# ScalarE applies the norm's weights while it rounds, and VectorE makes the low half in one pass

## What is computed

```python
def rmsnorm(x, w):
    xf = x.astype(jnp.float32)
    y = xf * lax.rsqrt(jnp.mean(xf * xf, axis=-1, keepdims=True) + EPS)
    return (y * w.astype(jnp.float32)).astype(x.dtype)

# layer 0:  rmsnorm(x, e_norm)  @ e_w_in
# layer 1:  rmsnorm(x, o_norm)  @ o_w_in
# layer 2:  rmsnorm(rmsnorm(x, final_norm), norm_mix_w) @ w_in
# layer 3:  rmsnorm(h, norm_ffn_w) @ ffn_w_up
```

## Time and profile before

| | us |
|---|---|
| median of 3 runs | 3475.65 (3473.97 to 3477.48) |
| the profiled execution | 3474.76, its span 3472.6 |
| PE busy | 3231.7 (93%) |
| VectorE busy | 2320.0 (67%) |
| ScalarE busy | 1833.2 (53%) |
| POOL busy | 687.3 (20%) |
| first norm with its blocks | from 13 to 48 us |
| norms of layers 1, 2 and 3 | 669 to 807, 1454 to 1597, 2669 to 2740 us |

### The profile page before, as it was taken

The page is one execution under the profiler, slowest core; times in us unless marked ns, Lnnn a source line. Parts: engine busy times, 40 slices in busy tenths (PEclk is TensorE's granted clock), DMA queues, the critical chain, the costliest instruction groups (busy, mean ns, idle before and its releaser), DMA issues.

```text
span 3472.6 us, 54222 instructions
## 1 busy us (share of the span) xinstructions
PE 3231.7 (93%) x21710; PEld 2944.0 (85%) x21710; DVE 2320.0 (67%) x3235; ACT 1833.2 (53%) x2370; POOL 687.3 (20%) x1118
## 2 busy tenths in 40 slices
PE   6999878999999899998998988998999999999998
PEld 6889878888888888887877877888999888888887
DVE  7655767656666776667666766666656788888544
ACT  5544667544665555654555444333444566666443
POOL 2000000010000000012676775776000100000000
PEclk9999988999999999999999999988999999999999
DMA  5435333555444445555433333333555555555554
GB/s 189 141 134 180 126 109 132 191 188 195 163 156 156 151 152 174 173 188 199 158 105 115 129 121 121 132 131 128 199 184 183 188 192 189 189 191 191 188 188 140
DMA packets 158046, 560.54 MB, mean 161 GB/s; under 512 B 17552, under 2 KB 25808, under 8 KB 157152
## 3 DMA queue, kind: packets, MB, share of 16 engines
q1 hardware_dynamic: 157792, 557.06, 47.6%
HBM read 550.64 MB, written 6.36 MB: 160 GB/s over the span
## 4 chain that ended last, share of the span: by engine, by line
PE 68%; DVE 12%; POOL 10%; ACT 6%; issue 3%; DMA 1%; DVEq 0%; ACTq 0%; POOLq 0%; SPq 0%
PE ps L555 68%; POOL TB L1906 5%; DVE WL L1309 3%; POOL PT L1906 2%; ACT WH L890 2%; POOL BX L1906 2%; ACT L880 1%; POOL BS L1906 1%; POOL SQ L1906 1%; DVE XV L1283 1%; DVE XC L1283 1%; DVE BS L1299 0%; DVE X L1283 0%; DMA RAW<-in_w 0%; ACT SQ L880 0%
## 5 line engine op out<-in xcount | busy, mean ns | idle before, releaser
L555 PE MATMUL ps<-XN,WH 128*128 128x256 f32 (+1 forms) x8864 | 1901.3, 308 | 54.2 <-DVE XN L1272 20.0
L890 ACT ACTIVATE WH<-RAW 128x1024 fp32r<-128x1024 f32 x1010 | 1065.1, 1058 | 1309.2 <-PE ps L555 1276.8
L1309 DVE TENSOR_TENSOR WL<-RAW,WH 128x1024 fp32r<-128x1024 f32 x1010 | 1260.9, 1253 | 518.7 <-ACT WH L890 512.4
L555 PEld LDWEIGHTS ps<-XN,WH 128*128 128x128 f32 x8864 | 1468.2, 197 | 144.8 <-issue 22.2
L555 PE MATMUL ps<-XN,WL 128*128 128x256 f32 x5120 | 1461.8, 285 | 0.0
L555 PEld LDWEIGHTS ps<-XN,WL 128*128 128x128 f32 x5120 | 999.8, 195 | 0.0
L555 PE MATMUL ps<-YS,WH 128*128 128x512 f32 (+1 forms) x1088 | 377.7, 392 | 31.6 <-DVE ZB L1272 29.4
L1906 POOL TENSOR_TENSOR RSB<-RSB,SQ 128x256 f32<-128x256 f32 x75 | 87.5, 1166 | 1244.1 <-ACT SQ L880 1243.1
L555 PE MATMUL ps<-YS,WL 128*128 128x256 f32 x1056 | 296.5, 281 | 0.0
L555 PEld LDWEIGHTS ps<-YS,WH 128*128 128x128 f32 x1088 | 203.9, 190 | 81.9 <-DVE ZB L1272 32.3
L1906 POOL TENSOR_TENSOR SQ<-SQ 128x256 f32<-128x256 f32 (+1 forms) x32 | 37.8, 1182 | 1129.5 <-ACT SQ L880 1127.5
(11 more groups left out here) (327 smaller groups left out, 3423.3 us busy)
## 6 DMA issues: line engine op xcount, KB each, us to landing
RAW<-in_w SPq DMA_DIRECT2D x1010, 512.0 KB, 3.3
CSB<-sums SPq DMA_DIRECT2D x64, 128.0 KB, 3.7
scratch<-X SPq DMA_DIRECT2D x2, 2048.0 KB, 7.8
X<-scratch SPq DMA_DIRECT2D x2, 2048.0 KB, 7.7
X<-in_x SPq DMA_DIRECT2D x4, 512.0 KB, 7.9
X<-in_x SPq DMA_DIRECT2D x1, 2048.0 KB, 7.9
out<-X SPq DMA_DIRECT2D x4, 512.0 KB, 2.6
WIF<-in_w_if SPq DMA_DIRECT2D x1, 576.0 KB, 14.3
```

The source lines that it names most:

```text
L555: return pe.e.matmul(dst, l, r, start=start, stop=stop, skip_group_check=True)
L890: act.e.activation(WH[:, w % NH, :], RAW[:, w % NB, :], ACT.Copy).then_inc(*act.one(("wh", w)))
L1309: dve.e.tensor_tensor(WL[:, w % NB, :], RAW[:, w % NB, :], WH[:, w % NH, :].bitcast(F32), SUB).then_inc(*dve.one(("wl", w)))
```

## The change

ScalarE reads x itself and multiplies by the norm's weights, a column of 128, as it rounds. VectorE then computes x times weight minus the high half in a single scalar_tensor_tensor. TMP and TMP0 are gone (X keeps its place), and so are the marks `xw` and `xf`; the new mark `xa` says that X has its sum. For layer 2 the product of final_norm and norm_mix is made once (FW), and the square of x times final_norm takes the weight as the square's scale. ScalarE waits for the vectors (CV) ahead of its first instruction, and in `norm0` for the tiles of x. `st1` waits for `xa` in place of `xw`. In `norm0`, VectorE's low half now stands at the step of its own tile; in `project` it stands one tile later, as before.

```diff
--- before.py
+++ after.py
@@ -361,6 +361,7 @@
         RST = fx("RST", 2)
         TRI = fx("TRI", 384)
         EPSC = fx("epsc", 1)
+        FW = fx("FW", 16)
         R0 = fx.at

 
@@ -370,7 +371,6 @@
         w1 = m.at
         m = Map(nc, w1 + 5120, end)
         X0 = v3(m("X0", 16 * 256), 16)
-        TMP0 = v3(m("TMP0", 512), 2)
         m = Map(nc, R0, end)
         XMS = [v3(m(f"XMS{i}", 4 * 512, F32R), 4) for i in range(2)]
         XCS = [v3(m(f"XCS{i}", 4 * 512, F32R), 4) for i in range(2)]
@@ -407,7 +407,7 @@
         RS2 = m("RS2", 256)
         SPT = [m(f"SPt{i}", 16) for i in range(3)]
         m = Map(nc, XT, end)
-        TMP = v3(m("TMP", 512), 2)
+        m.at += 2048
         X = v3(m("X", 16 * 256), 16)

 
@@ -526,6 +526,10 @@
             w = dict(SHP)[name]
             return CS[rows, SOFF[name] + c:SOFF[name] + c + (n or w)]

+        def norm_w(L, k):
+
+            return FW[:, k:k + 1] if L == 2 else cv(["e_norm", "o_norm", "", "norm_ffn"][L], k)
+
         ident, ones = cs("ident"), cs("ones")
         LAYER = {"e_w_in": 0, "o_w_in": 1, "w_in_2": 2, "ffn_w_up_2": 3}

@@ -889,24 +893,27 @@
                         act.wait_ge(*at("used", w - NH))
                     act.e.activation(WH[:, w % NH, :], RAW[:, w % NB, :], ACT.Copy).then_inc(*act.one(("wh", w)))

-            def square(key, n, acc, slot, x):
+            def square(key, n, acc, slot, x, scale=1.0):
                 if n == 0:
-                    fn(acc, x, ACT.Square, (*key, 0))
+                    fn(acc, x, ACT.Square, (*key, 0), scale=scale)
                 else:
                     if n > 2:
                         act.wait_ge(*at(key[0][:-1], key[1], n - 2))
-                    fn(SQ4[:, slot + n % 2, :], x, ACT.Square, (*key, n))
-
-            def norm_tile(L, k, x, tmp):
+                    fn(SQ4[:, slot + n % 2, :], x, ACT.Square, (*key, n), scale=scale)
+
+            def norm_tile(L, k, x):
+                fn(XN[:, k, 0:256], x[:, k, :], ACT.Copy, ("xh", L, k), scale=norm_w(L, k))
+                square(("sqr", L), k, RSB, 0, x[:, k, :])
                 if L == 2:
-                    act.wait_ge(*at("xf", L, k))
-                    square(("sq1r", L), k, RS1, 2, tmp[:, k % 2, :])
-                act.wait_ge(*at("xw", L, k))
-                fn(XN[:, k, 0:256], tmp[:, k % 2, :], ACT.Copy, ("xh", L, k))
-                square(("sqr", L), k, RSB, 0, x[:, k, :])
+                    square(("sq1r", L), k, RS1, 2, x[:, k, :], cv("final_norm", k))

             def norm0(k):
-                norm_tile(0, k, X0, TMP0)
+                act.wait_ge(*at(f"x0{k // 4}"))
+                norm_tile(0, k, X0)
+
+            def project(L, kind, n):
+                act.wait_ge(*at("xa", L, n))
+                norm_tile(L, n, X)

             def rsqrt(dst, src, n, *names):
                 fn(dst, src, ACT.Ln, bias=EPSC, scale=1.0 / n)
@@ -1045,7 +1052,7 @@
                     fn(YS1[:, 16 + 4 * h:20 + 4 * h, 0:256], HB, ACT.Copy, ("yhh", h))

             def eo(n, s):
-                norm_tile(1, n, X, TMP)
+                project(1, "eo", n)

             def dts(s):
                 if s == 0:
@@ -1092,7 +1099,7 @@
                     fn(YS2[:, 4 * g:4 * g + 4, 0:256], YB, ACT.Copy, ("y2h", g))

             def oo(n, s):
-                norm_tile(2, n, X, TMP)
+                project(2, "oo", n)

             def s5c(s):
                 lr, dt, mag, th, r, s1, c1, den, fr_, fi_ = P1
@@ -1225,7 +1232,7 @@
                     fn(MS[:, n, 0:256], VB[:, n % 2, :], ACT.Copy, ("msh", n))

             def wo(n, s):
-                norm_tile(3, n, X, TMP)
+                project(3, "wo", n)

             def up(i, s_, s):
                 vg, k = VG[i % 2], 43 * s_ + i
@@ -1256,6 +1263,7 @@
                 rsqrt(RSB, bank("nsum", 4)[:, 0:256], 2048, ("rs", 4))

             act.wait_ge(*at("eps"))
+            act.wait_ge(*at("cv"))
             walk(lambda t, k, a, b: None, unit, {
                 "norm0": norm0, "nend": nend, "nend2": nend2, "xm": xm, "k": k_, "v": v, "o": o, "gates": gates, "z": z,
                 "lruc": lruc, "xl": xl, "zl": zl, "ra": ra, "ix": ix, "tail": tail, "heads": heads, "eo": eo, "dts": dts,
@@ -1327,26 +1335,13 @@
                 for t in range(taps - 2, -1, -1):
                     stt(dst, src[:, t:t + 256], w(t), dst, MUL, ADD, *(names if t == 0 else ()))

-            def norm_rest(L, k, tmp):
+            def norm_rest(L, k, x):
                 dve.wait_ge(*at("xh", L, k))
-                rest(XN[:, k, :], tmp[:, k % 2, :], ("xn", L, k))
-
-            def norm_tile(L, k, x, tmp, w):
-                t = tmp[:, k % 2, :]
-                if L == 2:
-                    ts(t, x[:, k, :], cv("final_norm", k), None, MUL, None, ("xf", L, k))
-                    dve.wait_ge(*at("sq1r", L, k))
-                    ts(t, t, cv(w, k), None, MUL, None, ("xw", L, k))
-                else:
-                    ts(t, x[:, k, :], cv(w, k), None, MUL, None, ("xw", L, k))
-                if k:
-                    norm_rest(L, k - 1, tmp)
-                if k == 15:
-                    norm_rest(L, k, tmp)
+                stt(XN[:, k, 256:512], x[:, k, :], norm_w(L, k), XN[:, k, 0:256].bitcast(F32), MUL, SUB, ("xn", L, k))

             def norm0(k):
                 dve.wait_ge(*at(f"x0{k // 4}"))
-                norm_tile(0, k, X0, TMP0, "e_norm")
+                norm_rest(0, k, X0)

             def softplus_mid(t1, t2):
                 ts(t2, t1, 1.0, None, ADD, None)
@@ -1360,6 +1355,7 @@

             def consts():
                 dve.wait_ge(*at("cs"))
+                tt(FW, cv("final_norm", 0, 16), cv("norm_mix", 0, 16), MUL)
                 ts(TRI, cs("mask"), 0.0, None, ALU.is_ge, None)

             def xm(h, j, s):
@@ -1510,15 +1506,18 @@
                     dve.wait_ge(*at("yhh", h))
                     rest(YS1[:, 16 + 4 * h:20 + 4 * h, :], HB, ("ysh", h))

-            def project(L, kind, n, load, w):
+            def project(L, kind, n, load):
                 dve.wait_ge(*at("tile", kind, n))
                 dve.wait_ge(*at(load))
                 tt(X[:, n, :], X[:, n, :], bank(kind, n)[:, 0:256], ADD)
-                tt(X[:, n, :], X[:, n, :], bank(kind, n)[:, 256:512], ADD, ("free", kind, n))
-                norm_tile(L, n, X, TMP, w)
+                tt(X[:, n, :], X[:, n, :], bank(kind, n)[:, 256:512], ADD, ("free", kind, n), ("xa", L, n))
+                if n:
+                    norm_rest(L, n - 1, X)
+                if n == 15:
+                    norm_rest(L, n, X)

             def eo(n, s):
-                project(1, "eo", n, "x1", "o_norm")
+                project(1, "eo", n, "x1")

             def dt(s):
                 dve.wait_ge(*at("st1"))
@@ -1594,7 +1593,7 @@
                     rest(YS2[:, 4 * g:4 * g + 4, :], YB, ("y2", g))

             def oo(n, s):
-                project(2, "oo", n, "x2", "norm_mix")
+                project(2, "oo", n, "x2")

             def nend2():
                 dve.wait_ge(*at("rsa", 2))
@@ -1849,7 +1848,7 @@
                     rest(MS[:, n, :], VB[:, n % 2, :], ("ms", n))

             def wo(n, s):
-                project(3, "wo", n, "x3", "norm_ffn")
+                project(3, "wo", n, "x3")

             def ffn0():
                 dve.wait_ge(*at("rs", 3))
@@ -2017,7 +2016,7 @@
                 load(X, args["x"], "x1")

             def st1():
-                sp.wait_ge(*at("xw", 1, 15))
+                sp.wait_ge(*at("xa", 1, 15))
                 load(scratch, X, "st1")

             def csb(h):
```

## The result

The changed kernel takes 3466.27 us in the median of 8 runs (3464.04 to 3468.58); the kernel before, in 8 runs beside it, 3476.58 (3473.97 to 3477.48). The profiled execution of the changed kernel took 3468.58, the slowest of its eight; its span of 3466.8 is 5.8 us under that of before (3472.6). So this trace shows only a part of what the medians show.

The account below looks back on a forecast made before the run. PE was taken as the bound, full in three of four normalizations, leaving the start and two seams: 1.5 + 0.4 + 0.3 = 2.2 us, so 3472.6 for the profiled execution, median 3473.4, range 3469.5 to 3477.2.

Parts of the forecast that it names:

- what FW costs: One added product of 16 columns for normalization 2, some 0.2 us, at a point where VectorE waits anyway.
- (d): Rival: PE's half-clock stretches elsewhere shift with the start, either way, several us, 3467 to 3484; chance 0.08.
- The start: First normalization: earlier first matmul, new VectorE order and shorter units together bring 1.5 us, ends at 0.35 and 2.8.
- this first start: PE's first matmul comes at 12.6 instead of 13.00, some 0.35 to 0.4 us sooner.
- let the clock fall: First normalization: row 5 taken at half clock, unit 2 ending at 27.1; had the clock held, 26.1.
- block row 5: First normalization: it waits for XN 5 behind two WL (3.45 us together) and begins near 24.5.
- The steady loop: Units 3 to 6 of the first normalization: about 4.0 us each instead of 4.1, some 0.5 over four.
- The rule of the Trainium skill: VectorE's new instruction on even tiles waits out POOL's addition: a unit takes 4.07 us, the start sum is 1.2.
- The seam behind normalization 1: X's scratch store goes out 0.4 us earlier and PE's later idle shrinks by 0.4; bounds 0 and 0.4.
- The seam behind normalization 2: The chain shortens by near one microsecond, of which 0.3 us counts; bounds 0 and 0.3.
- Normalizations 1 to 3 stay full of matmuls: PE has no idle in these three stages, so VectorE's or ScalarE's savings there are off the path.
- VectorE's 36 us: Work VectorE loses over the kernel, 36 us less; off the path in the three full stages.

Follow-up runs that it names:

- e1: The kernel before with 16 unused columns (64 bytes) ahead of R0, no instruction changed: 3466.03 us, ratio 0.9971 to the kernel before.
- e2: The changed kernel with FW written over norm_mix in CV, so that R0 and all addresses stay as before: 3472.36 us.
- e9: The changed kernel with XN moved up 32 bytes and R0 192 in all: 3447.77 us, ratio 0.9921 to the kernel before.
- e4: The kernel before with 8 idle columns (32 bytes) ahead of R0: 3478.17 us, ratio 1.0008 to the kernel before.
- e5: The kernel before with 32 idle columns (128 bytes) ahead of R0: 3482.90 us, ratio 1.0018 to the kernel before.
- e10: The kernel before with WH, XN and everything from R0 on moved up 64 bytes, RAW and WL staying: 3475.16 us, ratio 1.0000.

## Why the prediction was wrong

**Failed: what FW costs.** The prediction said of the sixteen columns "One tiny product (16 columns) is added once, some 0.2 us", and the text ahead of it says that X keeps its place. It priced the instruction and not the bytes: it set the effect of the 64 bytes on PE's full stages at nothing, without a reason, and e1 measured them at 9.5 us of the 10.3. Each of its terms rests on PE's full stages keeping their length, "Whatever VectorE or ScalarE save or lose there is off the path". That is right of the engines beside PE, but the stages got shorter by PE itself. No rival holds this; (d), the half-clock stretches, was given 3467 to 3484 and not for this reason. The measured time lies under its low end too.

**The start: right in kind, too small, and partly luck.** PE's timeline of the changed kernel, its waits in the first norm and the first sum of squares:

```profile
23.96 0.51 PE L559 MATMUL ps<-XN,WH 128*128 128x256 f32 x2 [1.69 <-DVE XN L1291]
27.94 0.51 PE L559 MATMUL ps<-XN,WH 128*128 128x256 f32 x2 [0.84 <-DVE XN L1291]
...
44.69 0.67 PE L559 MATMUL ps<-RSB,CS 128*128 128x256 f32 x2 [1.72 <-POOL RSB L1905]
...
24.00:28.00 4.00, 3.16 (x25) 2.96 (x25) 3.72 (x4) 2.85 (x5) 0.74 (x2) 1.00 0.29 97
```

PE's first matmul is at 12.61 (12.6 forecast), but that is luck: it lies between 12.48 and 13.15 in the kernels with the change and between 12.73 and 13.12 in those without (13.00 in the trace of before), so the traces don't show the 0.35 to 0.4 us forecast. The sum of squares is 3.2 us earlier, where 1.5 were forecast; 0.4 of it is this first start, the rest two things. The clock is one: behind the idle 1.69 us it stays at 1.00, where it was 0.55 behind 2.02 us before; by the table above that is worth 1.0 us in the new order, as the prediction had priced it before it let the clock fall. It is no property of the change, since in e1, which has before's instructions, the clock also read 1.00 behind 2.01 us of idle. The other is block row 5, at 23.96 here and 23.80 in e2 where my walk had 24.5, and so 0.5 to 0.7 us sooner: the two WL ahead of it took 2.90 us and not 3.45, a stretched duration that I had carried over from the earlier trace rows. A unit takes 3.97 us ((39.85 - 23.96)/4) where I had said 4.0.

The steady loop, in the changed kernel's chain that ended last (start, us, what):

```profile
23.96 1.72 PE ps L559 x12
...
25.76 1.07 ACT WH L894
...
26.86 0.52 ACT XN L884
...
27.40 0.50 DVE XN L1291
...
27.94 1.71 PE ps L559 x12
```

It is the odd tile that closes it, 1.72 + 1.07 + 0.52 + 0.50 and the small gaps between, and not the even one beside POOL's addition. My walk had the two within 0.1 us of each other and picked the other. The rule of the Trainium skill on a port held for the whole length (page "SBUF — State Buffer", section "Who interferes with whom") would have made it 4.07 a unit; the instruction that it delays isn't on the path here, so 3.97 says nothing on it. What does agree with it is the product FW, with two inputs in SBUF: it lasts 717 ns for 16 columns and ends with POOL's addition beside it (44.58 and 44.56 us).

**The seam behind normalization 1: too large.** PE's timeline of the changed kernel, answering to the earlier trace rows:

```profile
825.97 0.36 PE L717 MATMUL ps<-CS,ZB 64*128 64x64 f32 x1 [5.22 <-DVE ZB L1307]
```

PE idles 5.22 us for 5.38, so 0.16 came back of 0.4. The store is issued earlier, but PE reaches this place earlier as well. The wait is 5.73 in e2 and 6.39 in e9, which have the change, and 5.15 in e1, which has not: the term is no larger than its scatter.

**The seam behind normalization 2: right.** POOL's last addition takes 0.74 us at 1589.26, against 1.69, and PE works on until the sum stands next, with no wait for POOL on its weight load, where it had waited 0.32 us. How much of that reached the end of the kernel no run shows by itself.

**Normalizations 1 to 3 stay full of matmuls:** right, as the stretches above show. VectorE's 36 us, 33.7 in fact, were worth nothing there: in e2, where the data stay, the three output projections differ from before by 0.1 us or less.

**Rival (d) is at work, beside the cause.** Between the sum of squares behind norm 2 and the stage of the gated products stand 5650 matmuls. They took 920 us before and in e1, 926 in the changed kernel's profiled execution, 923.5 in e2's. The rows, before and changed:

```profile
1596.00:2516.00 920.00, 823.72 (x5651) 749.55 (x5650) 594.81 (x835) 414.10 (x545) 558.92 (x1001) 0.93 0.41 138
```

```profile
1589.00:2515.00 926.00, 831.06 (x5652) 756.12 (x5651) 593.29 (x834) 413.80 (x545) 558.78 (x1002) 0.92 0.41 137
```

The granted clock is 0.92 for 0.93, PE busy 7.3 us longer over the same matmuls. One place shows it plainly: behind a wait of 3.00 us for ZS in both kernels, the same blocks run at the full clock before and at 0.70 in the changed kernel, which costs 2.1 us.

```profile
2469.50:2475.50 6.00, 6.00 (x53) 6.00 (x52) 2.17 (x4) 1.82 (x3) 0.00 (x0) 1.00 0.94 350
```

```profile
2467.00:2475.10 8.10, 8.10 (x51) 8.10 (x51) 1.92 (x4) 1.78 (x3) 0.00 (x0) 0.70 0.89 322
```

So this trace shows 5.8 us of gain and not 10; its execution also lies 2.3 us over the median. From the sum of squares behind norm 2 to the first block on ZS, all six traces with the change have 3.7 to 4.3 us more than before; those without it have -1.4 to 1.6 in five cases, 3.0 in e4 and 4.5 in e5. Whether the change itself makes the clock fall there more often is open: there is one trace of each kernel, and it was not tried.

## What to carry to other kernels

An added tile has two prices, its instruction and its bytes. When an edit adds, drops or resizes a buffer, compare the addresses of everything laid out behind it, and time the old kernel with dead columns of that size before the gain is credited to the edit. In a kernel bound by PE, count matmuls in a few stretches where PE is full and the clock is 1.00, before and after: that number, good to 0.1%, showed in one profile what no busy share and no wait did. And a pad of a few columns ahead of each large operand is a cheap knob: here it gave more than the rewrite. It has to be tried, since no rule for the best place came out of these runs.

## What the hardware showed

- Blocks of the same matmuls at the same granted clock of 1.00, PE without idle time, took 346.7, 350.0, 351.1 or 353.3 ns in the mean (512 and 256 columns, down projection) and 350.1 to 359.9 ns (three of 256 columns), as the tiles were laid out relative to each other in SBUF, in steps of 32 or 64 bytes. Over the kernel that is some -24 us at the best layout tried (e9 against e2) and +7 at the worst (e5).
- Moving all tiles together changed nothing (0.9998, 0.9989 to 1.0006). Moves by 64 and 192 bytes of the moving tiles were alike for the down projection, those by 0 and by 128 were not.
- A total that stands still can hide some 10 us lost and as much won in its stages: e10.
- An idle stretch of PE of 2.0 us at the start was followed by a granted clock of 0.55 in one execution (before) and of 1.00 in another (e1), with the same instructions. The clock that stayed up was no gain there: the next idle stretch of 2.00 us was followed by 0.68, and the first sum of squares came 0.8 us later.
- POOL's addition took 0.74 us at 1589.26, where VectorE was idle, and 1.69 in the earlier trace rows, where VectorE made a WL beside it.
